# Moving the low parts of the stick-breaking weights from VectorE to GpSimd, by way of a raw copy

## What is computed

```
def stick_breaking_block(start, q, k, v):
    z = jnp.einsum('bqhd,bkhd->bhqk', qb, k) * (D_HEAD ** -0.5)
    visible = (s[None, :] < t[:, None])[None, None]
    log_not = jnp.where(visible, -jax.nn.softplus(z), 0.0)
    suffix = lax.cumsum(log_not, axis=3, reverse=True)
    excl = jnp.concatenate([suffix[..., 1:], jnp.zeros_like(suffix[..., :1])], axis=-1)
    a = jnp.where(visible, jnp.exp(jax.nn.log_sigmoid(z) + excl), 0.0)
    return jnp.einsum('bhqk,bkhd->bqhd', a, v)
...
merged = gate_sb * (o_sb @ w_branch_sb) + gate_ds * (o_ds @ w_branch_dsa)
return merged @ w_out
```

## Time and profile before

| | |
|---|---|
| median of 3 runs | 1843.07 us (1842.69 to 1844.76) |
| profiled execution, its own time | 1841.95 us |
| its span in the trace | 1840.2 us |
| busy: PE, DVE, ACT, POOL | 96%, 56%, 38%, 22% of the span |

### The profile page before, as it was taken

One profiled execution on the slowest core, in us unless ns is written; L12 is line 12 of the kernel. 1 busy time (PEld: TensorE's weight loads), 2 busy tenths in 40 slices (PEclk: granted clock), 3 DMA queues, 4 the chain that ended last, 5 costly groups with the idle time before them and its releaser, 6 DMA issues. The chain is left out here.

```text
span 1840.2 us, 25612 instructions
## 1 busy us (share of the span) xinstructions
PE 1761.6 (96%) x10056; PEld 1495.7 (81%) x10056; DVE 1023.2 (56%) x1764; ACT 703.2 (38%) x1375; POOL 398.4 (22%) x174
## 2 busy tenths in 40 slices
PE   5999999999999999899999899999999999999998
PEld 4889888899877788788878688888888888888886
DVE  5387888999999997577744254323222222222225
ACT  5366444444444443799932233302111121203032
POOL 1111212321111111111014500404132222314033
PEclk9999999999999999899999899999999999999999
DMA  4564424423423323444134432302020211112023
GB/s 166 162 188 138 130 78 126 143 93 98 111 73 104 101 74 96 113 94 94 42 114 150 161 116 79 92 12 80 12 80 25 68 46 46 57 35 76 17 75 143
DMA packets 65583, 170.54 MB, mean 93 GB/s; under 512 B 9320, under 2 KB 23976, under 8 KB 65464
## 3 DMA queue, kind: packets, MB, share of 16 engines
q1 hardware_dynamic: 65464, 168.91, 30.5%
HBM read 126.47 MB, written 42.41 MB: 92 GB/s over the span
## 5 line engine op out<-in xcount | busy, mean ns | idle before, releaser
L594 PE MATMUL bk<-x_hi,w_hi 128*128 128x512 f32 (+2 forms) x832 | 308.6, 371 | 1.2 <-PEq L284 1.2
L594 PE MATMUL bk<-x_lo,w_hi 128*128 128x512 f32 (+2 forms) x832 | 298.2, 358 | 0.0
L594 PE MATMUL bk<-x_hi,w_lo 128*128 128x512 f32 (+2 forms) x832 | 297.6, 358 | 0.0
L265 POOL TENSOR_TENSOR w_lo<-w_raw,w_hi 128x1024 fp32r<-128x1024 f32 x53 | 131.4, 2480 | 478.1 <-ACT w_hi L261 478.1
L1370 ACT ACTIVATE relu<-bank 128x1024 f32<-128x1024 f32 x32 | 33.0, 1030 | 504.5 <-PE bank L1281 504.5
L1281 PE MATMUL bank<-m_hi,w_hi 128*128 128x512 f32 x512 | 199.5, 390 | 0.0
L1281 PE MATMUL bank<-m_hi,w_lo 128*128 128x512 f32 x512 | 199.2, 389 | 0.0
L1281 PE MATMUL bank<-m_lo,w_hi 128*128 128x512 f32 x512 | 199.2, 389 | 0.0
L935 DVE TENSOR_SCALAR_CACHE_REDUCE sel<-sc,st_bits 128x272 bf16<-128x272 f32 (+6 forms) x217 | 184.2, 890 | 0.9
L1451 DVE TENSOR_TENSOR acc<-acc,bank 128x1024 f32<-128x1024 f32 x56 | 68.4, 1221 | 192.5 <-PE bank L1257 191.6
L594 PEld LDWEIGHTS bk<-x_hi,w_hi 128*128 128x128 f32 x832 | 158.7, 191 | 17.0 <-issue 1.3
(11 more groups left out here) (177 smaller groups left out, 3586.9 us busy)
## 6 DMA issues: line engine op xcount, KB each, us to landing
w_raw<-w_units SPq DMA_DIRECT2D x99, 512.0 KB, 3.8
raw<-w_units SPq DMA_DIRECT2D x24, 512.0 KB, 3.5
k_hi<-k_d SPq DMA_DIRECT2D x32, 260.0 KB, 5.4
k_lo<-k_d SPq DMA_DIRECT2D x32, 260.0 KB, 6.0
q_st<-q_d SPq DMA_DIRECT2D x32, 256.0 KB, 4.6
g_d<-stage_hi SPq DMA_DIRECT2D x32, 256.0 KB
gate<-g_d SPq DMA_DIRECT2D x16, 512.0 KB, 4.4
v_raw<-v_d SPq DMA_DIRECT2D x16, 260.0 KB, 7.2
```

The lines of the kernel that those rows point to most:

```text
L265: pool.tensor_tensor(w_lo[:, s], w_raw[:, s], w_hi[:, s].bitcast(F32), ALU.subtract).then_inc(lo_done, 1)
L594: mm = pe.matmul(pj[b][:, 0:c1 - c0], w[:, s, kt, :], a[:, kt, c0:c1], start=kt == 0 and k == 0, stop=kt == KT - 1 and k == 2)
```

## The change

For the jobs of SB, ACT copies each of the first two groups of transposed weights twice: raw into the job's own `a_buf` slot (whose weights have been transposed by then), and rounded into `pt_hi` as before. The second copy frees the bank (`sb_hi`). POOL then makes `pt_lo` from the two SBUF copies (`sb_lo`), in its queue between the chunk work of the step's two parts. DVE leaves these groups out; the third group of a 1040-key job (one tile), the values and all of DS stay on DVE. `product` waits for `sb_lo`, and ACT, before it writes the slot again in step j+3 (`sticks`, in the first steps of DS `exponent`), too. Groups per head: one for blocks 0 to 2, two for blocks 3 to 7, so 13, and 104 in all (64 of them 128x512).

```diff
@@ -123,6 +123,9 @@
     if j_ % NB == 4 and j_ // NB + 1 < 2 * H:
         for half_ in range(2):
             tp_take(("v", j_ // NB + 1, half_), j_)
+SB_GROUPS = sorted(n_ for key_, n_ in TPN.items() if key_[0] == "p" and key_[1] < NJ // 2 and key_[2] < 2)
+SB_NO = {n_: k_ for k_, n_ in enumerate(SB_GROUPS)}
+DVE_NO = [n_ - sum(r_ < n_ for r_ in SB_GROUPS) for n_ in range(len(TP_BANK))]
 TP_PREV = [max([m_ for m_ in range(n_) if TP_BANK[m_] == b_], default=None) for n_, b_ in enumerate(TP_BANK)]
 
 
@@ -432,6 +435,7 @@
             z_ready, zs_used, zd_used = sem("f_z"), sem("f_zsused"), sem("f_zdused")
             scan_done, a_done, exp_done, recip = (sem("f_" + n) for n in ("scan", "a", "exp", "recip"))
             tp_ready, tp_hi, tp_free = sem("f_tp"), sem("f_tphi"), sem("f_tpfree")
+            sb_hi, sb_lo = sem("f_sbhi"), sem("f_sblo")
             pv_done, o_free, oh_done = sem("f_pv"), sem("f_ofree"), sem("f_oh")
             o_spilled = [sem("f_ospill0"), sem("f_ospill1")]
             or_in, or_hi, or_lo = [sem("f_orin0"), sem("f_orin1")], sem("f_orhi"), sem("f_orlo")
@@ -553,14 +557,32 @@
 
             @block.gpsimd
             def _(pool):
-                for u in range(U_BRANCH):
-                    for n in range(FIRST_CHUNK[u], LAST_CHUNK[u] + 1):
-                        if u >= U_STEP and n in LO_NO:
-                            b, w = n % 2, CHUNK[n][2] - CHUNK[n][1]
-                            pool.wait_ge(hi_evac, n + 1)
-                            pool.tensor_tensor(stage_lo[:, b, 0:w], stage_lo[:, b, 0:w].bitcast(F32), stage_hi[:, b, 0:w].bitcast(F32),
-                                               ALU.subtract).then_inc(lo_evac, 1)
+                def rest_chunk(n):
+                    u = CHUNK[n][0]
+                    if n in LO_NO:
+                        b, w = n % 2, CHUNK[n][2] - CHUNK[n][1]
+                        pool.wait_ge(hi_evac, n + 1)
+                        pool.tensor_tensor(stage_lo[:, b, 0:w], stage_lo[:, b, 0:w].bitcast(F32), stage_hi[:, b, 0:w].bitcast(F32),
+                                           ALU.subtract).then_inc(lo_evac, 1)
+                    if n == LAST_CHUNK[u]:
+                        rest_unit(pool, u + 2, u % 2)
+
+                def rest_turned(j):
+                    for k, tiles in enumerate(groups(JOBS[j][2])[:2]):
+                        dst = (slice(None), j % 2, slice(4 * k, 4 * k + len(tiles)), slice(None))
+                        raw = a_buf[:, j % 3, 512 * k:512 * k + len(tiles) * P].rearrange("p (c k) -> p c k", c=len(tiles))
+                        pool.wait_ge(sb_hi, SB_NO[TPN["p", j, k]] + 1)
+                        pool.tensor_tensor(pt_lo[dst], raw, pt_hi[dst].bitcast(F32), ALU.subtract).then_inc(sb_lo, 1)
+
+                for u in range(U_STEP):
                     rest_unit(pool, u + 2, u % 2)
+                for j in range(STEPS + 2):
+                    for n in ENDS[j][0]:
+                        rest_chunk(n)
+                    if j >= 2:
+                        rest_turned(j - 2)
+                    for n in ENDS[j][1]:
+                        rest_chunk(n)
                 for j in range(NJ // 2 + 1, NJ + 6):
                     for p in range(4):
                         if j == RELOAD[p] + 2:
@@ -606,8 +628,10 @@
                               stop=True).then_inc(s_ready, 1)
 
                 def turn_bank(n):
-                    if TP_PREV[n] is not None:
-                        pe.wait_ge(tp_free, TP_PREV[n] + 1)
+                    if TP_PREV[n] in SB_NO:
+                        pe.wait_ge(sb_hi, SB_NO[TP_PREV[n]] + 1)
+                    elif TP_PREV[n] is not None:
+                        pe.wait_ge(tp_free, DVE_NO[TP_PREV[n]] + 1)
                     elif TP_BANK[n] < 2:
                         bank_read(NC_ALL - 2 + (TP_BANK[n] + NC_ALL) % 2)
 
@@ -663,7 +687,11 @@
                     tiles = [x_ for g_ in groups(i) for x_ in g_]
                     for m, (c, r) in enumerate(tiles):
                         if m % 4 == 0:
-                            pe.wait_ge(tp_free, TPN["p", j, m // 4] + 1)
+                            n = TPN["p", j, m // 4]
+                            if n in SB_NO:
+                                pe.wait_ge(sb_lo, SB_NO[n] + 1)
+                            else:
+                                pe.wait_ge(tp_free, DVE_NO[n] + 1)
                         for k, (v, w) in enumerate(((v_hi, pt_hi), (v_hi, pt_lo), (v_lo, pt_hi))):
                             mm = pe.matmul(bk[o_bank(j)][0:DH, 0:P], v[0:r, g % 2, c, :], w[0:r, j % 2, c, :], start=m == 0 and k == 0,
                                            stop=m == len(tiles) - 1 and k == 2)
@@ -752,6 +780,7 @@
                         act.wait_ge(z_ready, z + 1)
                         if m == 0 and j >= 3:
                             act.wait_ge(tp_ready, TPN["p", j - 3, len(groups(JOBS[j - 3][2])) - 1] + 1)
+                            act.wait_ge(sb_lo, SB_NO[TPN["p", j - 3, min(1, len(groups(JOBS[j - 3][2])) - 1)]] + 1)
                         act.activation(a_buf[:, j % 3, c0:c1], src, ACT.Sigmoid, scale=DH ** -0.5)
                         if m == 0 and j >= 2:
                             act.wait_ge(a_done, j - 1)
@@ -763,6 +792,8 @@
                     s, keys = j % 2, KEYS[i]
                     act.wait_ge(zd_used, Z_END[j] - NZ_SB)
                     act.wait_ge(tp_ready, TPN["p", j - 3, len(groups(JOBS[j - 3][2])) - 1] + 1)
+                    if JOBS[j - 3][0] == SB:
+                        act.wait_ge(sb_lo, SB_NO[TPN["p", j - 3, min(1, len(groups(JOBS[j - 3][2])) - 1)]] + 1)
                     act.activation(a_buf[:, j % 3, 0:keys], n_buf[:, s, 0:keys], ACT.Exp, scale=-1.0, bias=small[:, 16 + s:17 + s],
                                    accum_out=small[:, 20 + j % 4:21 + j % 4]).then_inc(exp_done, 1)
 
@@ -779,7 +810,12 @@
                         act.wait_ge(tp_ready, n + 1)
                         if k == 0 and j >= 2:
                             act.wait_ge(pv_done, j - 1)
-                        act.copy(pt_hi[:, j % 2, 4 * k:4 * k + m, :], bk[TP_BANK[n]][:, 0:m * P].rearrange("p (c k) -> p c k", c=m)).then_inc(tp_hi, 1)
+                        src = bk[TP_BANK[n]][:, 0:m * P].rearrange("p (c k) -> p c k", c=m)
+                        if n in SB_NO:
+                            act.copy(a_buf[:, j % 3, 512 * k:512 * k + m * P].rearrange("p (c k) -> p c k", c=m), src)
+                            act.copy(pt_hi[:, j % 2, 4 * k:4 * k + m, :], src).then_inc(sb_hi, 1)
+                        else:
+                            act.copy(pt_hi[:, j % 2, 4 * k:4 * k + m, :], src).then_inc(tp_hi, 1)
 
                 def round_values(g):
                     for half in range(2):
@@ -1025,7 +1061,9 @@
                     t, g, i = JOBS[j]
                     for k, tiles in enumerate(groups(i)):
                         n, m = TPN["p", j, k], len(tiles)
-                        dve.wait_ge(tp_hi, n + 1)
+                        if n in SB_NO:
+                            continue
+                        dve.wait_ge(tp_hi, DVE_NO[n] + 1)
                         dst = (slice(None), j % 2, slice(4 * k, 4 * k + m), slice(None))
                         dve.tensor_tensor(pt_lo[dst], bk[TP_BANK[n]][:, 0:m * P].rearrange("p (c k) -> p c k", c=m), pt_hi[dst].bitcast(F32),
                                           ALU.subtract).then_inc(tp_free, 1)
```

## The result

The changed kernel took 1845.74 us (median of 22 runs, 1843.73 to 1849.43) against 1842.86 us for the kernel before (22 runs, 1841.16 to 1844.76). The ratio is 1.0017 with a 95% interval from 1.0011 to 1.0023: slower by 0.17%, 2.9 us, less than the 0.2% that was called "no change" in the prediction, but clear of noise, and not the 2 us of gain that was forecast.

What follows compares the result with a forecast made beforehand. PE was taken to bound the stretch (535.5 of 547 us busy), with only 6.0 us of waits to be had from DVE. The terms -4.7 + 1.3 + 1.4 gave -2.0 us, a median of 1841.1 us, range 1837.1 to 1847.

Steps and rivals of the forecast that it cites:

- no change: Whole kernel: differences within about 0.2%, 3.7 us, were taken as not distinguishable; chance of landing within, 0.57.
- The gain: PE's eight L622 waits for the values' second bank: 4.7 of 6.0 us saved by the bank's earlier release.
- DVE's relief: 104 subtractions leaving DVE, 59 us: by itself worth nothing, as PE waits for DVE nowhere else in the stretch.
- The busy times: In the stretch of the change: DVE near 465 us, POOL near 240, ACT near 290.
- POOL's queue: Starts of steps 8 and 16: POOL's unit work first, subtraction 0.4 and 0.9 us late, costing PE 1.3 us.
- the exclusion of the two: DVE and POOL holding each other up: cost 0, since DVE's scan would come soon after the sigmoids.
- rival B: POOL and DVE exclude each other before three-chunk scores: 1845.0 us for two boundaries, 1854.8 for all seven; chance 0.13.
- the sum: Whole kernel: -4.7 + 1.3 + 1.4 = -2.0 us, median 1841.1 us; chance 0.52.
- The seam: Between SB and DS: ACT's doubled copies delay the next head's load and PE by 1.4 us, bounds 0.7 and 2.5.
- A: Costs at POOL and the seam don't land: -4.7, at most -6.0 us, 1838.4 to 1837.1 us; chance 0.25.
- C: DVE becomes the bound through collisions with POOL, by up to 21 us: 1859 us; chance 0.04.
- D: The bank comes no earlier, ACT being late by its new work; only costs stay: +2.7 us, 1845.8; chance 0.06.

Runs made afterwards that it cites:

- e4: Changed kernel with jobs 5, 13 and 61 to 63 kept as in the kernel before (97 of 104 groups changed); 1837.93 us, ratio 0.9973 to before.
- e11: Kernel before with raw copies on ACT for 16 groups of the eight 912-key jobs, DVE subtracting from SBUF, POOL nothing new; 1836.43 us, ratio 0.9972.
- e2: Changed kernel with jobs 5 and 13 (one group each) kept on DVE as in the kernel before; 1840.73 us, ratio 0.9986 to before.
- e3: Changed kernel with jobs 61 to 63, those at the seam, kept as in the kernel before; 1840.72 us, ratio 0.9994 to before.
- e5: Kernel before with the change for jobs 5 and 13 alone (two groups of 104); 1846.9 us, ratio 1.0025 to before.
- e6: Kernel before with the change for jobs 61 to 63 alone, those at the seam; 1843.58 us, ratio 1.0006 to before.
- e9: Changed kernel in full, but POOL makes the turned weights' low parts ahead of the first part's chunk work; 1841.24 us, ratio 0.9996 to the kernel before.
- e1: Kernel before with the change for the eight 912-key jobs alone, both groups (16 of 104); 1836.1 us, ratio 0.9966 to before.
- e10: Kernel before with the change for only the first group of the eight 912-key jobs (8 of 104); 1837.73 us, ratio 0.9973 to before.
- e7: Kernel before with two constant copies on ACT as a pure delay ahead of the first sigmoid of steps 8, 16, ..., 56; 1861.98 us, ratio 1.0106.
- e8: Kernel before with ACT's 104 raw copies added but read by nobody, the subtraction staying on DVE from the bank; 1847.47 us, ratio 1.0028.

## Why the prediction was wrong

**The gain was right, mechanism and size.** It said 4.7 of 6.0 us, with 0.7 us left at step 12 and 0.1 at seven others. Left were 0.63 and seven times 0.09 us, 1.2 in all, and with the other places left out (e4) PE's idle time in SB is 4.7 us shorter. That DVE's relief is worth nothing in itself is shown by e11, whose DVE is as full as before.

**The busy times were right** for DVE (465 forecast, 464.7) and POOL (240; 241.4), and a little high for ACT (290; 277): copies one behind the other overlap, as the two in 1.07 us of the earlier trace rows against 0.61 us for one do.

**The step that failed is the one on POOL's queue**: "At step 8 it is free at 262.96 and done at 264.25, against 263.88: 0.4 us late ... PE passes both on in full: 1.3 us." The place and the mechanism were right, and step 16 nearly so (0.9 forecast, 0.98 measured). Two things were mis-sized. First, at step 8 the wait grew by 1.43 us and not by 0.4, because DVE's scan got ahead of POOL and POOL's subtraction took 1.0 us longer. The prediction had priced the exclusion of the two at 0, since DVE would "make its scan soon after the sigmoids, away from POOL's turn"; at this step it did not, because POOL's weight unit held DVE up just before. That is rival B's mechanism, at one of the seven boundaries. Second, and larger, a wait of PE was priced by its length, and the sum has no term for the clock, without a reason given. The wait of 2.01 us brought a clock fall, 1.5 to 1.9 us more (changed less e2, e3 less e4, e5 less before). Together 3.9 to 4.3 us stand where 1.3 was put. With that alone the sum -4.7 + 1.3 + 1.4 becomes about +0.8.

Of the first, the trace of before had the lesson. The rows on the exclusion show what POOL and DVE do to each other. At step 8 DVE's scan, 0.02 us ahead, took its usual 1.25 us and POOL's subtraction 1.0 us more than its own 1.29; in the earlier trace rows POOL was ahead and DVE's multiply was the long one. "SBUF — State Buffer" of the Trainium skill says in "Who interferes with whom" that whoever issues first wins; both places agree.

Two readings in the prediction were off, without effect on the sum. The waits of 6.1 and 6.0 us are not the 11.5 us of idle time: the first wait of 2.0 us began at 192.0, ahead of the stretch, and one of 0.4 us at step 64 was left out. And the row at 332.89 us in the earlier trace rows is search work; the scan that rival B and the 1.25 us rest on starts at the same instant and was not shown:

```profile
332.89 1.25 DVE L993 TENSOR_TENSOR_SCAN n_buf<-n_buf 128x528 f32<-128x528 f32 x1
```

**The seam was right in its mechanism and short in size**: the output came 1.39 us later (1.4 forecast) and, in e6, PE with it. Over three traces of each kernel the seam is 1.8 us longer. The spread over traces of before is 0.8 us, so the 0.4 us beyond may be chance.

**The end of the selected attention was not in the prediction at all.** There PE waits 1.04 us for DVE (to 935.5 us before, to 936.9 in the changed kernel), and behind it the clock falls in the changed kernel and not in the kernel before. The change has no operation there; it only shifts when PE works and waits ahead of it. The fall came in every trace of the changed kernel and in no other; e9 has one behind the next wait. e2 and e6 have the seam's shift and e3 and e5 that of jobs 5 and 13, each without the fall. So it is neither alone, and why it comes is not settled. The fall in e9 is a reason why e9 is not the 3 us faster than before that its SB and seam promise.

**The rivals.** A (no costs) was wrong for this kernel, but e4 is it: 1837.9 us, as A said. B acted at one boundary, not at all seven. C and D were wrong: DVE was never late by a step, and the bank came earlier. The range, up to 1847, held the time; the sign of the forecast did not. That the time is D's 1845.8 and near B's 1845.0 for two boundaries is chance: D had the whole gain missing, B had no clock in it.

**The version to keep** is e1, e10 or e11, 5 to 6 us faster than before (0.27 to 0.34%), not told apart. e11 is the plainest: a raw copy on ACT for the steps in which the bank is wanted at once, and nothing on POOL.

## What to carry to other kernels

Apply an edit where the trace shows the wait and nowhere else: 8 of 104 groups gave the gain, and 2 others took most of it back. When work goes to another engine, read that engine's queue at the moment of each use, and look for the one step in which something long stands ahead; averages of 44% busy say nothing of it. And price a wait of PE that is left or added above its length: behind the waits of 1.35 to 2.99 us inside SB a clock fall came 11 times in 25 (counted in the last section), at some 1.6 us each. Compare PE's idle time between two fixed matmuls, not only the length: here it repeated to 0.03 us where the length moved by 1.2.

## What the runs showed of the hardware

The granted clock fell behind four of seven waits that were alike (e7, 2.1 us each), at 1.6 us of time for each fall. At step 8 it fell behind the wait of 2.01 us in all five traces that have it, at step 16 behind the wait of 1.57 us in none of the same five. At step 4 it fell behind the wait of 2.44 us in one of six traces and not behind the 2.99 us of e8, and at step 12 of e8 behind 1.35 us. Whether it falls is thus not told by the length of the wait alone. At step 8 the fall began 0.2 to 1.5 us behind the wait's end, not at a fixed distance. "TensorE: Matmul & The Clock Gate" of the Trainium skill, section "What's actually happening", has the clock depend on recent activity at instants that run free of the kernel; this spread agrees.

POOL's exclusion reached operations of DVE that nobody would count as heavy: a comparison of 7 columns with two SBUF inputs took 2.32 us beside POOL's 2.40 us, where it takes 0.17 alone. The profile shows this as a long operation and not as a wait. In the kernel before and in the changed kernel, at step 8:

```profile
262.93 0.17 DVE L939 TENSOR_TENSOR st_bits<-st_bits 128x7 f32<-128x7 f32 x1
...
258.66 2.32 DVE L975 TENSOR_TENSOR st_bits<-st_bits 128x7 f32<-128x7 f32 x1
```
